# Delta scan: the state update of a pair's two heads spread over all four quadrants of the array

## The reference, cut to what matters

```
def wkv7_scan(S0, r, w, k, v, a, b):
    def step(S, inp):
        r_t, w_t, k_t, v_t, a_t, b_t = inp
        sa = jnp.einsum('bhij,bhj->bhi', S, a_t)
        S = S * w_t[:, :, None, :] + sa[..., None] * b_t[:, :, None, :] + v_t[..., None] * k_t[:, :, None, :]
        return S, jnp.einsum('bhij,bhj->bhi', S, r_t)
    S, ys = lax.scan(step, S0, seqs)
    return S, jnp.moveaxis(ys, 0, 1)
```

## Time and profile before

| what | value |
|---|---|
| median of three runs | 3739.11 us |
| profiled execution: span | 3727.5 us |
| time around the span (3739.11 less 3727.5) | 11.6 us |
| TensorE matmuls busy | 3466.0 us, 93% of the span |
| VectorE busy | 1553.3 us, 42% |
| ScalarE busy | 1130.6 us, 30% |
| `delta_scan`'s steps | 2310 to 2489 us of the span |

### The profile page before, as it was taken

The page is one execution under the profiler, slowest core; times in us unless marked ns, Lnnn a source line. Parts: engine busy times, 40 slices in busy tenths (PEclk is TensorE's granted clock), DMA queues, the critical chain, the costliest instruction groups (busy, mean ns, idle before and its releaser), DMA issues. The chain is left out here.

```text
span 3727.5 us, 61420 instructions
## 1 busy us (share of the span) xinstructions
PE 3466.0 (93%) x26430; PEld 3253.3 (87%) x26430; DVE 1553.3 (42%) x2525; ACT 1130.6 (30%) x2105; POOL 610.8 (16%) x713
## 2 busy tenths in 40 slices
PE   8899979999999999998899884776999999999998
PEld 8888769989999999994698783765998999999997
DVE  6335473343332332325246667556334332232233
ACT  6223263233211211226345421544223321121123
POOL 1000112002100100121221366422100210010012
PEclk9999989999999999997999997998999999999999
DMA  6422312102111111116546666963210111111111
GB/s 225 108 59 66 105 34 77 43 18 46 51 46 46 46 46 46 44 31 206 191 157 221 199 176 143 227 142 93 91 29 23 46 46 46 46 46 47 46 43 66
DMA packets 457389, 323.16 MB, mean 87 GB/s; under 512 B 105134, under 2 KB 435214, under 8 KB 453870
## 3 DMA queue, kind: packets, MB, share of 16 engines
q1 hardware_dynamic: 402874, 280.72, 26.3%
q10 hardware_dynamic: 43876, 18.99, 2.0%
q0 software_dynamic: 10368, 19.51, 1.6%
HBM read 232.29 MB, written 86.96 MB: 86 GB/s over the span
## 5 line engine op out<-in xcount | busy, mean ns | idle before, releaser
L83 PE MATMUL ps<-am_y,am_wh 128*128 128x352 f32 x4944 | 1182.0, 322 | 12.4 <-PEq L2567 12.4
L83 PE MATMUL ps<-am_h,am_wh 128*128 128x352 f32 x3648 | 886.4, 325 | 1.2 <-DVE am_h L1410 1.2
L83 PEld LDWEIGHTS ps<-am_y,am_wh 128*128 128x128 f32 x4944 | 855.5, 188 | 14.7 <-issue 13.4
L83 PE MATMUL ps<-am_y,am_wl 128*128 128x352 f32 x2472 | 792.2, 320 | 0.0
L83 PEld LDWEIGHTS ps<-am_h,am_wh 128*128 128x128 f32 x3648 | 638.7, 188 | 4.3 <-DVE am_h L1410 1.4
L83 PE MATMUL ps<-am_h,am_wl 128*128 128x352 f32 x1824 | 589.7, 323 | 0.0
L83 PEld LDWEIGHTS ps<-am_y,am_wl 128*128 128x128 f32 x2472 | 463.7, 188 | 0.0
L83 PEld LDWEIGHTS ps<-am_h,am_wl 128*128 128x128 f32 x1824 | 343.7, 188 | 0.0
L1498 POOL TENSOR_TENSOR am_silu<-am_silu,rs 128x352 f32<-128x352 f32 x132 | 126.9, 963 | 1229.2 <-ACT am_silu L1354 1229.2
L1080 DVE TENSOR_TENSOR x<-ps,x 128x352 f32<-128x352 f32 x240 | 125.9, 525 | 463.4 <-PE ps L83 457.8
L83 PE MATMUL ps<-rw_parts,rw_wh 128*128 128x352 f32 (+1 forms) x1152 | 289.4, 333 | 22.8 <-PEq L2549 13.0
(11 more groups left out here) (327 smaller groups left out, 4592.5 us busy)
## 6 DMA issues: line engine op xcount, KB each, us to landing
am_w<-in_ffn_w SPq DMA_DIRECT2D x120, 512.0 KB, 3.9
rw_ra_d<-tb_rk SPq DMA_DIRECT2D x8, 1056.0 KB, 7.8
rw_kbt_d<-tb_gk SPq DMA_DIRECT2D x8, 1056.0 KB, 4.0
rw_gg_d<-tb_gk SPq DMA_DIRECT2D x8, 1056.0 KB, 6.2
fr_w<-in_xa_wk SPq DMA_DIRECT2D x8, 1024.0 KB, 5.6
fr_w<-in_xa_wv SPq DMA_DIRECT2D x8, 1024.0 KB, 5.5
am_w<-in_xa_wq SPq DMA_DIRECT2D x16, 512.0 KB, 4.1
am_w<-in_xa_wo SPq DMA_DIRECT2D x16, 512.0 KB, 4.1
```

The lines of the kernel that those rows point to most:

```text
L83: mm = nc.tensor.matmul(out, l, part, start=start and n == 0, stop=stop and n == 2)
```

## The change

In odd pairs the two heads change places in k (`kbt`), g, v and u: their rows of head 0 stand on the upper 64 partitions and head 1's on the lower ones. The state, z, y, ra and the decay stay as they were. With that the update of an odd pair's head h reads rows of side 1 - h and still writes columns of side h, so four matmuls in a row of L571 lie in (low, low), (high, high), (high, low) and (low, high). Its results go to four PSUM banks, two for each q, where they went to two, and VectorE's add reads them as it reads u. L563 writes its columns in the other order for odd pairs. ScalarE opens g out with four instructions of half the size (even and odd pairs apart) instead of two; g's buffer has another layout. `tables` stores kbt and g with two DMAs of 64 rows each in place of one of 128, and v's rows go to the swapped places.

```
-        g, ra = (sb(s, 2, PAIRS, 2, 2, C) for s in ("g", "ra"))
+        g, ra = sb("g", 2, 2, PAIRS, 2, C), sb("ra", 2, PAIRS, 2, 2, C)
-        ROWS, REST, OPENS = 2, 3, 4
+        ROWS, REST, OPENS = 2, 3, 6
...
-                            mm = nc.tensor.matmul(ps[side[h], 2 + 2 * q + p % 2, at:at + HD], tt[r, l % SLOTS, h, sub, p // 2, :],
+                            mm = nc.tensor.matmul(ps[side[h ^ p % 2], 2 + 2 * q + p % 2, at:at + HD], tt[r, l % SLOTS, h, sub, p // 2, :],
                                                   z[r, p // 2, :], start=True, stop=True)
...
-                            r, at = side[h], p % 4 * HD
-                            mm = nc.tensor.matmul(ps[r, 2 + 2 * q, at:at + HD], kbt[r, l % SLOTS, p, sub, :], vu[r, p, :],
+                            r, at = side[h ^ p % 2], p // 2 % 2 * HD
+                            mm = nc.tensor.matmul(ps[side[h], 2 + 2 * q + p % 2, at:at + HD], kbt[r, l % SLOTS, p, sub, :], vu[r, p, :],
                                                   start=True, stop=True)
...
-                    nc.vector.tensor_tensor(half(S, q), bank(2 + 2 * q), half(S, q), ALU.add).then_inc(s_added, 1)
+                    nc.vector.tensor_tensor(by_side(S, q), sides(q), by_side(S, q), ALU.add).then_inc(s_added, 1)
...
-                for t, src in ((g, g_in), (ra, ra_in)):
-                    for h in range(2):
-                        nc.scalar.activation(t[:, n % 2, :, :, h], src[:, l % SLOTS, :, sub, :]
-                                             .rearrange("r p (a t) -> r p a t", a=2), ACT.Copy, scale=of_head[:, h:h + 1])\
+                for h in range(2):
+                    for e in range(2):
+                        nc.scalar.activation(g[:, n % 2, :, e::2, h ^ e], g_in[:, l % SLOTS, e::2, sub, :]
+                                             .rearrange("r p (a t) -> r a p t", a=2), ACT.Copy, scale=of_head[:, h:h + 1])\
                             .then_inc(opened, 1)
+                for h in range(2):
+                    nc.scalar.activation(ra[:, n % 2, :, :, h], ra_in[:, l % SLOTS, :, sub, :]
...
+        rows_of = lambda p, h, n=HD: slice((h ^ p % 2) * n, ((h ^ p % 2) + 1) * n)
...
-                    sp.dma_start(vt_d[p, h * C:(h + 1) * C, half::2, :], vts[r:r + C, 0:n, :]).then_inc(vt_stored, 16)
+                    sp.dma_start(vt_d[p, rows_of(p, h, C), half::2, :], vts[r:r + C, 0:n, :]).then_inc(vt_stored, 16)
...
-                    sp.dma_start(kbt_d[p], kbt[:]).then_inc(kbt_stored, 16)
+                    for h in range(2):
+                        sp.dma_start(kbt_d[p, rows_of(p, h)], kbt[h * HD:(h + 1) * HD]).then_inc(kbt_stored, 16)
                     sp.wait_ge(g_out, len(PIECES) * (p + 1))
-                    sp.dma_start(g_d[p], gs[:]).then_inc(g_stored, 16)
+                    for h in range(2):
+                        sp.dma_start(g_d[p, rows_of(p, h)], gs[h * HD:(h + 1) * HD]).then_inc(g_stored, 16)
```

More of the change, by code:

```diff
@@ L544, in _ @@
                 for q in range(2):
-                    z_part(q, lambda p: g[:, s, p, 0], lambda p: v[:, l % SLOTS, p, sub, :], True)
+                    z_part(q, lambda p: g[:, s, 0, p], lambda p: v[:, l % SLOTS, p, sub, :], True)
                 for q in range(2):
@@ L569, in _ @@
                         for h in range(2):
-                            r, at = side[h], p % 4 * HD
-                            mm = nc.tensor.matmul(ps[r, 2 + 2 * q, at:at + HD], kbt[r, l % SLOTS, p, sub, :], vu[r, p, :],
+                            r, at = side[h ^ p % 2], p // 2 % 2 * HD
+                            mm = nc.tensor.matmul(ps[side[h], 2 + 2 * q + p % 2, at:at + HD], kbt[r, l % SLOTS, p, sub, :], vu[r, p, :],
                                                   start=True, stop=True)
                     mm.then_inc(s_done, 1)
-                y_part(n, lambda p: vu[:, p, :], lambda p: g[:, s, p, 1], False).then_inc(y_done, 1)
+                y_part(n, lambda p: vu[:, p, :], lambda p: g[:, s, 1, p], False).then_inc(y_done, 1)
             pe.wait_ge(state_ready, 2 * N)
@@ L595, in _, with by_side, sides @@
             dve.wait_ge(init_set, 2)
+            def by_side(t, q):
+                return half(t, q).rearrange("r (a e) i -> r e a i", e=2)
+            def sides(q):
+                return ps[:, 2 + 2 * q:4 + 2 * q, 0:2 * HD].rearrange("p e (a i) -> p e a i", i=HD)
             for n in range(N):
@@ L604, in _ @@
                     dve.wait_ge(u_done, 2 * n + q + 1)
-                    by_side = lambda t: half(t, q).rearrange("r (a e) i -> r e a i", e=2)
-                    u = ps[:, 2 + 2 * q:4 + 2 * q, 0:2 * HD].rearrange("p e (a i) -> p e a i", i=HD)
-                    nc.vector.tensor_tensor(by_side(vu), u, by_side(v[:, l % SLOTS, :, sub, :]), ALU.add)\
+                    nc.vector.tensor_tensor(by_side(vu, q), sides(q), by_side(v[:, l % SLOTS, :, sub, :], q), ALU.add)\
                         .then_inc(u_out, 1)
@@ L629, in open_out @@
                     act.wait_ge(y_done, n - 1)
-                for t, src in ((g, g_in), (ra, ra_in)):
-                    for h in range(2):
-                        nc.scalar.activation(t[:, n % 2, :, :, h], src[:, l % SLOTS, :, sub, :]
-                                             .rearrange("r p (a t) -> r p a t", a=2), ACT.Copy, scale=of_head[:, h:h + 1])\
+                for h in range(2):
+                    for e in range(2):
+                        nc.scalar.activation(g[:, n % 2, :, e::2, h ^ e], g_in[:, l % SLOTS, e::2, sub, :]
+                                             .rearrange("r p (a t) -> r a p t", a=2), ACT.Copy, scale=of_head[:, h:h + 1])\
                             .then_inc(opened, 1)
+                for h in range(2):
+                    nc.scalar.activation(ra[:, n % 2, :, :, h], ra_in[:, l % SLOTS, :, sub, :]
+                                         .rearrange("r p (a t) -> r p a t", a=2), ACT.Copy, scale=of_head[:, h:h + 1])\
+                        .then_inc(opened, 1)
             def empty(n):
@@ L1901, in load_triangles @@
             else:
-                sp.wait_ge(g_stored, 16 * PAIRS)
-                sp.wait_ge(kbt_stored, 16 * PAIRS)
+                sp.wait_ge(g_stored, 32 * PAIRS)
+                sp.wait_ge(kbt_stored, 32 * PAIRS)
             sp.dma_start(inv_m[q].rearrange("l a s t -> l a (s t)"), lt_of(lt_d, q)).then_inc(inv_in[q], 16)
@@ L2015, in _ @@
             sp.wait_ge(vt_stored, 64 * PAIRS)
-            for t in (ra_stored, g_stored, kbt_stored):
-                sp.wait_ge(t, 16 * PAIRS)
+            sp.wait_ge(ra_stored, 16 * PAIRS)
+            sp.wait_ge(g_stored, 32 * PAIRS)
+            sp.wait_ge(kbt_stored, 32 * PAIRS)
             for b in range(BLOCKS):
@@ L2191, in put_kbt @@
                 if i == 0:
-                    act.wait_ge(kbt_stored, 16 * p)
+                    act.wait_ge(kbt_stored, 32 * p)
                 act.wait_ge(kbt_done, len(PIECES) * p + i + 1)
@@ L2315, in put_g @@
                 if i == 0:
-                    dve.wait_ge(g_stored, 16 * p)
+                    dve.wait_ge(g_stored, 32 * p)
                     dve.wait_ge(lt_stored, 32 * p)
```

## The result

The changed kernel takes 3763.43 us (median of four runs, 3753.53 to 3765.94); the kernel before took 3739.18 beside it. The ratio is 1.0066, 95% interval 1.0052 to 1.0080: 0.66% slower, some 24 us, well over what a measurement can tell. The forecast was 3735.1 and its range ended at 3741.

The account below looks back on a forecast made before the run. The scan was taken as bound by a ring through TensorE and VectorE, with many steps stopped by late code. Terms summed to 4.6 or 2.8 us, taken as 4.0: 3739.1 - 4.0 = 3735.1 us, range 3730 to 3741.

Parts of the forecast that it names:

- Stores in `tables`: SyncE's queue in `tables`: 16 more issues of 0.32 us hide in 83.0 us of waits; cost 0, 5 if all exposed.
- L571 on four quadrants: Scan's L571: 32 records take about 0.7 to 0.8 us instead of 1.15; an undisturbed step gains 0.2 us.
- the ring: Undisturbed scan step: L571's first half, VectorE on the state, L523's second half, L530, L563, vu; 4.39 to 4.19 us.
- Steps that wait for code: Scan steps where TensorE stops for late code: gain 3.5 or 2.0 us for 2360 to 2470 us, by two readings.
- nothing is gained: Rival: the four matmuls don't run together or longer stops give everything back; 3739 us, chance 0.17.
- The clock: Rival in the scan: more stops lower TensorE's clock, 1.1 us each fall, eight more falls give 3744 us; chance 0.12.
- ScalarE: Scan: four g halves take at most 1.56 us instead of 1.32, covered by idle time before L638; cost 0.
- VectorE's add: Scan: the state add gets vu's pattern at vu's size, one add taking 0.42 us; cost 0.
- The 11.6 us around the span: Whole kernel: the profiled span of 3727.5 us was read as 11.6 us under the median.
- stores exposed or ScalarE late: Remaining rival cases: `tables` stores exposed, or ScalarE late in the scan; chance 0.03 together.

Follow-up runs that it names:

- t1: Kernel before with kbt and g each stored by two DMAs of 64 rows, one per partition half, scan unchanged; ratio 1.0040.
- t11: Same change to the kernel before as t1, measured once more beside other runs; ratio 1.0054.
- t9: Kernel before with kbt and g stored in partition halves that change places for odd pairs, v's rows in their old places; ratio 1.0048.
- t6: Changed kernel's stores (halves of 64 rows, odd pairs' halves and v's rows crossed) with the scan of the kernel before; ratio 1.0064.
- t3: Changed kernel with kbt and g stored whole again, odd pairs' heads swapped by the cross matmuls' output half instead; ratio 1.0002.
- t12: Kernel before with only g stored in two partition halves of 64 rows, kbt stored whole; ratio 1.0000.
- t4: Kernel before with only ScalarE's part of the change, g opened by four instructions into the new layout; ratio 1.0004.
- t8: Kernel before with kbt and g each stored by two DMAs of 64 rows, cut by even and odd rows; ratio 0.9997.

## Why the prediction was wrong, step by step

- *Stores in `tables`, "cost 0, and if all were exposed 5".* This step failed. Each new issue was priced at 0.32 us by the row of a 128-row store, with "bytes and row length stay as they were", and the 83.0 us of slack on SyncE's queue as cover. The issue of a g half takes 1.97 us and its landing 9.1. The slack was the wrong cover too: SyncE still waits 77.3 us for the same releaser after (L1989), but the late party is not the issue, it is the landing that VectorE waits for before the next pair. Measured cost: 22.9 us in the profiles; by the ratios of t1, t11, t9 and t6 0.40 to 0.64%, 15 to 24 us and on average 19, of the 24 us of the result. So the term was put at 0 to 5 and is 15 to 24.
- *L571 on four quadrants.* Right in mechanism and size: 0.79 us for 32 records where 0.69 to 0.8 was said, the ring 0.20 shorter, VectorE's multiply late next. That both row halves write each of its banks has no price that shows: in L563 each bank gets writes from one row half only, and it takes 0.69, without the wait for vu in the middle. The rule of the Trainium skill, page TensorEngine Tiling (Array Packing), section Restrictions and Gotchas, that different row tiles can't access one PSUM bank simultaneously, would have left 1.15; the trace disagrees.
- *Steps that wait for code, 3.5 or 2.0 us of gain.* Not there. Stops grew by 5.7 us to 30.2, where 2 to 4 were said. t3 nets +0.02%, with an interval that takes in the rival "nothing is gained" and reaches no further than 0.07% of gain; 4.6 us would be 0.12%.
- *The clock.* The rival's mechanism happened: nine falls in the scan instead of three. Six more at 1.1 us each are 6.6, beside 5.7 of stops and against about 5 of quicker steps, near the 7.1 that the scan is longer. But the profile of before has the fewest falls of all: old scans show 4 to 7 in the other kernels (t12 six, t6 seven), new ones 5 to 11. On average it is three more, some 3 us, at which t3's ratio is still a tie.
- *ScalarE.* A g half takes up to 0.50 us where I had 0.39 (four take 1.70, not at most 1.56); before L646 there are still 0.65 to 1.05 us of idle time. Covered as said, with less margin. Whether it lengthens the stops is open (t4).
- *VectorE's add.* Cost 0, as said: 0.42 us.
- *The 11.6 us around the span* were a quick profiled run; they cancelled in the sum and did no harm.

The chance for "stores exposed or ScalarE late" was 0.03 and its price at most 5 us. The bound was the mistake: a store that reads one half of the partitions had no row in the trace, and I bounded it from a store that reads both. That the sign of the forecast was wrong is this term's doing; that no gain was left beside it, as t3 shows, is a second miss, of 0.1%, and its cause is open between the longer stops and ScalarE.

## What to carry to other kernels

A store that reads 64 neighbouring partitions is another thing than half of one over 128 (237 against 406 GB/s here): before cutting one by partition halves, look whether the same move can be made elsewhere (here by the output half of matmuls that run anyway, at 1.0002) or the cut be laid across the partitions (t8, at 0.9997). When issues are added to a queue, look for who waits for the landing behind them, not only for the slack of the queue. And where TensorE's code arrives late behind table loads, spreading these loads gives more than a quicker matmul: 0.34% against nothing.

## What the runs showed of the hardware that I had not expected

- Stores that read 64 rows of one partition half move 237 GB/s at a full share of the DMA engines, where 64 even or odd rows move 405 and 128 rows 406.
- Two stores of 528 KB from one partition half each land after 5.3 us (kbt) and 9.1 us (g), where one of 1056 KB over all partitions landed after 4.0 and 6.2; cut by even and odd rows, they land after 3.7 and 5.0.
- The slow transfer shows on the issuing side as well: issues on the queue grow from 0.32 to 1.97 us, and those of lt behind them from 1.32 to 2.17.
- Four fp32 matmuls of 64 x 64 in four quadrants reach 0.79 us for 32 records even with two row halves writing one bank; in two quadrants it was 1.15. In four quadrants with one row half to a bank (L563) it is 0.69.
- Leaving out the table loads gave 17.0 us; the stops went from 24.5 to 3.2 us. With loads, a stop ends 2.5 to 3.0 us after a packet of code has started.
